# Recurrence scores of two decay steps in one run of TensorE, in a 62,819-instruction two-layer kernel

## The reference, cut to what matters

```python
f = lb + (1.0 - lb) * jax.nn.sigmoid(f_logit)      # decay of each channel, per position
k = 1.0 - f
scores = einsum('bhtd,bhsd,bhtsd->bhts', qc, kc, decay)   # decay = exp(b_t - b_s), b the running sum of log f
o_intra = einsum('bhts,bhsv->bhtv', scores, vc)
o_inter = einsum('bhtd,bhdv->bhtv', qc * exp(b), state)
```

## Time and profile before

| | |
|---|---|
| median of three runs | 3675.24 us |
| the profiled execution, its time | 3676.9 us |
| its span, first to last instruction | 3675.2 us |
| granted clock of PE, mean | 0.996 |
| PE / PEld busy | 3627.0 / 3128.5 us (99% / 85%) |
| DVE, ACT, POOL busy | 2034.2, 1510.6, 685.9 us (55%, 41%, 19%) |
| transfers | 820.57 MB, 223 GB/s in the mean |

### The profile page before, as it was taken

One profiled execution on the slowest core, in us unless ns is written; L12 is line 12 of the kernel. 1 busy time (PEld: TensorE's weight loads), 2 busy tenths in 40 slices (PEclk: granted clock), 3 DMA queues, 4 the chain that ended last, 5 costly groups with the idle time before them and its releaser, 6 DMA issues.

```text
span 3675.2 us, 62819 instructions
## 1 busy us (share of the span) xinstructions
PE 3627.0 (99%) x25608; PEld 3128.5 (85%) x25608; DVE 2034.2 (55%) x3851; ACT 1510.6 (41%) x2753; POOL 685.9 (19%) x407
## 2 busy tenths in 40 slices
PE   9999999999999999999999999999999999999999
PEld 7889888978897988987788788888877899998998
DVE  4757635551645354556645665555566465545555
ACT  3332431231232364576566665444555422223222
POOL 2001130000000000233333321000000254414442
PEclk9999999999999999999999999999999999999999
DMA  8746686557655877866766665554533666666664
GB/s 300 283 180 248 240 302 251 202 211 241 218 218 193 281 255 246 284 229 221 260 230 229 218 240 179 166 169 148 174 139 121 227 247 235 232 233 230 233 236 184
DMA packets 215534, 820.57 MB, mean 223 GB/s; under 512 B 22096, under 2 KB 71504, under 8 KB 152144
## 3 DMA queue, kind: packets, MB, share of 16 engines
q1 hardware_dynamic: 215248, 816.57, 63.1%
HBM read 615.15 MB, written 201.33 MB: 222 GB/s over the span
## 4 chain that ended last, share of the span: by engine, by line
PE 93%; ACT 2%; DVE 2%; DMA 1%; issue 1%; SPq 0%; POOL 0%; DVEq 0%; ACTq 0%
PE bank L1649 89%; PE bank L1653 4%; DVE P L2894 0%; DMA KS<-Kd 0%; ACT slot L2145 0%; SPq L3165 0%; DVE Z1a L2544 0%; ACT L2261 0%; POOL slot L3119 0%; ACT P L2271 0%; DMA Ib<-in_masks_dram 0%; DVE P L2850 0%; DMA DV<-Vd 0%; ACT TP L2281 0%; DVE P L2900 0%
## 5 line engine op out<-in xcount | busy, mean ns | idle before, releaser
L1649 PE MATMUL bank<-slot,Z0b 128*128 128x512 f32 (+1 forms) x3504 | 702.5, 351 | 0.7 <-DVE R L2497 0.7
L1649 PEld LDWEIGHTS bank<-slot,Z0b 128*128 128x128 f32 x3504 | 560.0, 188 | 90.2 <-DVE R L2497 1.5
L1649 PE MATMUL bank<-Z1b,slot 128*128 128x512 f32 (+1 forms) x2568 | 609.9, 381 | 5.3 <-DVE Z1b L2544 5.3
L1649 PE MATMUL bank<-Z1a,slot 128*128 128x512 f32 (+1 forms) x2568 | 607.0, 380 | 6.8 <-POOL slot L3119 5.4
L1649 PEld LDWEIGHTS bank<-Z1a,slot 128*128 128x128 f32 x2568 | 447.5, 190 | 96.5 <-POOL slot L3119 4.5
L1649 PEld LDWEIGHTS bank<-Z1b,slot 128*128 128x128 f32 x2568 | 445.1, 189 | 94.8 <-DVE Z1b L2544 7.4
L3119 POOL TENSOR_TENSOR slot<-raw,slot 128x1024 fp32r<-128x1024 f32 x110 | 274.1, 2498 | 705.5 <-ACT slot L2145 705.3
L2497 DVE SCALAR_TENSOR_TENSOR R<-bank,small,R 128x512 f32<-128x512 f32 x352 | 261.6, 748 | 178.5 <-PE bank L1649 178.1
L2850 DVE TENSOR_SCALAR_CACHE_REDUCE P<-bank 128x512 f32<-128x512 f32 (+3 forms) x320 | 189.3, 608 | 215.5 <-PE bank L1649 214.5
L1649 PE MATMUL bank<-KS,DQ 128*128 128x512 f32 (+3 forms) x960 | 278.1, 388 | 7.5 <-ACT P L2262 3.3
L3137 POOL TENSOR_TENSOR Z0b<-AF,Z0b 128x512 fp32r<-128x512 f32 x88 | 132.7, 1508 | 804.7 <-ACT Z0b L2335 804.7
(11 more groups left out here) (267 smaller groups left out, 5509.0 us busy)
## 6 DMA issues: line engine op xcount, KB each, us to landing
slot<-Wd SPq DMA_DIRECT2D x350, 1024.0 KB, 5.5
Wd<-slot SPq DMA_DIRECT2D x130, 1024.0 KB, 7.7
raw<-in_wts_dram SPq DMA_DIRECT2D x210, 512.0 KB, 4.9
DQ<-Qd SPq DMA_DIRECT2D x192, 128.0 KB, 4.0
slot<-Wd SPq DMA_DIRECT2D x40, 512.0 KB, 6.1
DV<-Vd SPq DMA_DIRECT2D x60, 256.0 KB, 4.6
KS<-Kd SPq DMA_DIRECT2D x24, 512.0 KB, 7.3
KS<-Kd SPq DMA_DIRECT2D x24, 384.0 KB, 7.3
```

Of the source, the lines that this page charges most:

```text
L1649: return e.matmul(o, a, b, start=start, stop=stop, skip_group_check=True)
```

## The change: what it does

Two levels (2p and 2p+1) are now formed in one run p, so a unit has four runs and not eight. To have both levels' operands at once, the second query buffer `Qc` is added, and `Fb` serves as second key buffer once the decays have been used. DVE makes the second level's changed halves straight into the other buffer (`hgrn_decayed`), and ACT copies the two unchanged halves over (two copies per head and run, in runs 0 to 2). The level-0 product of queries and decays moves ahead of the first run. Runs 0 and 2 write banks 2 and 3, runs 1 and 3 banks 4 and 5, each level 128 columns of its own, so the masked copies of a run (`hg m`, `hgrn_merged`) no longer have to be done before the next run, and are placed behind it. ACT's three copies of levels 6 and 7 come together. Space for `Qc` comes from `small` (512 to 360 columns) and from `sg`, which now is the buffer `DG`. In the planner, a run waits for 900 ns of ACT and 2400 ns of DVE for each head. Of the pooling, the second half is now let in 1000 ns after the first half's transfer is expected to be done, where before it was let in when ACT's scaling was.

```diff
         for j in range(2):
-            t[j] = P.put(("hg k", u, j), ("dve", 1400))
-        for i, L in enumerate((0,) + LEVELS):
+            t[j] = P.put(("hg k", u, j), ("dve", 2100))
+        for p in range(4):
             x = max(t)
             yield x
             for j in range(2):
-                t[j] = P.put(("hg sc", u, i, j), ("pe", 400), after=x) + 200
+                t[j] = P.put(("hg sc", u, p, j), ("pe", 800), after=x) + 200
+            if 0 < p < 3:
+                for j in range(2):
+                    yield from self.hgrn_merged(u, p - 1, j)
             for j in range(2):
                 yield t[j]
-                t[j] = P.put(("hg l", u, i, j), ("dve", 2200 if L == 16 else 1350 if L <= 16 else 1050), after=t[j])
+                t[j] = P.put(("hg l", u, p, j), ("act", 900), ("dve", 2400 if p < 3 else 1200), after=t[j])
+            if p == 2:
+                for j in range(2):
+                    yield from self.hgrn_merged(u, p, j)
+                    t[j] = max(t[j], P.clock["dve"])
         yield ("ev", ("A", s, 2 * hp, 1))
         for j in range(2):
             yield t[j]
...
+
+    def hgrn_merged(self, u, p, j):
+
+        yield self.P.end["hg sc", u, p, j] + 200
+        self.P.put(("hg m", u, p, j), ("dve", 1500 if p == 2 else 700), after=self.P.end["hg sc", u, p, j] + 200)
...
             t = P.put(("pl w", s, j), ("dve", 2500 + 1500 * j))
             yield t
             t = yield from self.short(("pl mm", s, j), ("pe", 900), ("act", 690), after=t)
-            self.dma(("Y2 out", s, j), 262144, t)
+            t = self.dma(("Y2 out", s, j), 262144, t)
             P.put(("pl y", s, j))
-            yield t
+            yield t + 1000
...
+        def level_operands(i, j):
+
+            return (Qc if i in (1, 2, 5, 6) else Qb)[j], (Kb if i in (0, 1, 2, 5, 6) else Fb)[j]
+
+        def halves_of(b, L):
+
+            return b[:, :].rearrange("p (n two l) -> p n two l", two=2, l=L)
+
+        def level_scores(i, j):
+
+            w = 64 if i == 7 else 32
+            at = 128 * (i % 2)
+            b = bank[(4 if i // 2 % 2 else 2) + j]
+            return b[:, at:at + NT * w].rearrange("p (c t) -> p c t", c=NT)
...
+            def hgrn_scores(u, p, j):
+                if p == 0:
+                    pe.wait_ge(*dve_hg("hg k", u, j, "q"))
                     pe.wait_ge(*act_g("ev", ("A", u // 2, (24 if u % 2 else 6) + j)))
                     if u:
                         pe.wait_ge(*dve_hg("hg n", u - 1, j, "on"))
                 else:
-                    pe.wait_ge(*dve_hg("hg l", u, i - 1, j, "m" if i - 1 <= 5 else "q"))
-                    if i - 1 > 5:
-                        pe.wait_ge(*act_hg("hg l", u, i - 1, j))
-                for c in range(NT):
-                    if L <= 16:
+                    pe.wait_ge(*dve_hg("hg l", u, p - 1, j, "q"))
+                    pe.wait_ge(*act_hg("hg l", u, p - 1, j))
+                    if p > 1:
+                        pe.wait_ge(*dve_hg("hg m", u, p - 2, j, "1"))
+                    elif u:
+                        pe.wait_ge(*dve_hg("hg yT", u - 1, j))
+                for i in (2 * p, 2 * p + 1) if j == 0 else (2 * p + 1, 2 * p):
+                    q, k = level_operands(i, j)
+                    if i <= 5:
                         pairs = [(32 * g, 32 * g, 32) for g in range(4)]
                     else:
-                        pairs = [(0, 32, 32), (64, 96, 32)] if L == 32 else [(0, 64, 64)]
-                    for ks, qs, w in pairs:
-                        x = mm(A_[ks:ks + w, w * c:w * c + w], Kb[j][:, 128 * c + ks:128 * c + ks + w],
-                               Qb[j][:, 128 * c + qs:128 * c + qs + w], True, True)
-                x.then_inc(*pe_hg.inc("hg sc", u, i, j))
+                        pairs = [(0, 32, 32), (64, 96, 32)] if i == 6 else [(0, 64, 64)]
+                    for c in range(NT):
+                        for ks, qs, w in pairs:
+                            x = mm(level_scores(i, j)[ks:ks + w, c, :], k[:, 128 * c + ks:128 * c + ks + w],
+                                   q[:, 128 * c + qs:128 * c + qs + w], True, True)
+                x.then_inc(*pe_hg.inc("hg sc", u, p, j))
...
+            def hgrn_level(u, p, j):
+                act.wait_ge(*pe_hg("hg sc", u, p, j))
+                if p < 3:
+                    i = 2 * p + 2
+                    act.wait_ge(*dve_hg("hg l", u, p, j, "u"))
+                    (q, k), (q1, k1) = level_operands(i, j), level_operands(i + 1, j)
+                    L = LEVELS[i - 1]
+                    e.activation(halves_of(q1, L)[:, :, 0, :], halves_of(q, L)[:, :, 0, :], ACT.Copy)
+                    e.activation(halves_of(k1, L)[:, :, 1, :], halves_of(k, L)[:, :, 1, :], ACT.Copy).then_inc(
+                        *act_hg.inc("hg l", u, p, j))
                     return
...
+                for i, L, r in (6, 32, 0), (6, 32, 64), (7, 64, 0):
+                    x = e.activation(sv[r:r + L, :, r + L:r + 2 * L], level_scores(i, j)[r:r + L, :, :], ACT.Copy)
+                x.then_inc(*act_hg.inc("hg l", u, p, j))
...
+            def hgrn_decayed(u, i, j):
+
+                L = LEVELS[i - 1]
+                (q, k), (q1, k1) = level_operands(i, j), level_operands(i + 1 if i % 2 == 0 else i, j)
+                tl = tot(u, j, i - 1).rearrange("p (n two) -> p n two", two=2)
+                e.tensor_tensor(halves_of(q1, L)[:, :, 1, :], halves_of(q, L)[:, :, 1, :], bc(tl[:, :, 0], L, 2), ALU.mult)
+                e.tensor_tensor(tot(u, j, i), tl[:, :, 0], tl[:, :, 1], ALU.mult)
+                return e.tensor_tensor(halves_of(k1, L)[:, :, 0, :], halves_of(k, L)[:, :, 0, :], bc(tl[:, :, 1], L, 2), ALU.mult)
+
+            def hgrn_level(u, p, j):
+                dve.wait_ge(*pe_hg("hg sc", u, p, j))
+                if p:
+                    dve.wait_ge(*act_hg("hg l", u, p - 1, j))
+                hgrn_decayed(u, 2 * p + 1, j).then_inc(*dve_hg.inc("hg l", u, p, j, "u"))
+                if p == 3:
+                    return
+                dve.wait_ge(*dve_hg("hg l", u, p, j, "u"))
+                hgrn_decayed(u, 2 * p + 2, j).then_inc(*dve_hg.inc("hg l", u, p, j, "q"))
+
+            def hgrn_merged(u, p, j):
+                cv = Cb[j][:, :, :]
+                dve.wait_ge(*pe_hg("hg sc", u, p, j))
+                dve.wait_ge(*act_c("lmask"))
+                if p:
+                    dve.wait_ge(*dve_hg("hg m", u, p - 1, j, "1"))
+                    x = e.copy_predicated(cv, bc(lmask[:, 2 * p - 1, :], NT), level_scores(2 * p, j))
                 else:
-                    tl = tot(u, j, i - 1).rearrange("p (n two) -> p n two", two=2)
-                    qv = Qb[j][:, :].rearrange("p (n two l) -> p n two l", two=2, l=L)
-                    kv = Kb[j][:, :].rearrange("p (n two l) -> p n two l", two=2, l=L)
-                    e.tensor_tensor(qv[:, :, 1, :], qv[:, :, 1, :], bc(tl[:, :, 0], L, 2), ALU.mult)
-                    e.tensor_tensor(tot(u, j, i), tl[:, :, 0], tl[:, :, 1], ALU.mult)
-                    e.tensor_tensor(kv[:, :, 0, :], kv[:, :, 0, :], bc(tl[:, :, 1], L, 2), ALU.mult).then_inc(
-                        *dve_hg.inc("hg l", u, i, j, "q"))
-                cv = Cb[j][:, :, :]
-                sc = bank[2 + j][:, 0:128].rearrange("p (c t) -> p c t", c=NT)
-                sv = heads_of(Sb[j])
...
+                    x = e.tensor_tensor(cv, level_scores(0, j), id4, ALU.mult)
+                x.then_inc(*dve_hg.inc("hg m", u, p, j, "0"))
+                dve.wait_ge(*dve_hg("hg m", u, p, j, "0"))
+                e.copy_predicated(cv, bc(lmask[:, 2 * p, :], NT), level_scores(2 * p + 1, j)).then_inc(
+                    *dve_hg.inc("hg m", u, p, j, "1"))
+                if p == 2:
+                    sv = heads_of(Sb[j])
+                    dve.wait_ge(*dve_hg("hg m", u, p, j, "1"))
                     dve.wait_ge(*pool_c("zero"))
```

More of the change, by code:

```diff
@@ L1136, in build @@
         lamv = sb("lamv", [128, 8])
-        small = sb("small", [128, 512])
+        small = sb("small", [128, 360])
         raw = [sb(f"raw{i}", [128, 1024]) for i in range(NRAW)]
@@ L1178, in build @@
                    ("lmask", [128, 5, 32], U8)] + two("Cb", [128, NT, 32])
-                  + [x for n in ("Fb", "Kb", "Qb", "Gb", "Sb", "Tb") for x in two(n, [128, SUB])]
+                  + [x for n in ("Fb", "Kb", "Qb", "Qc", "Gb", "Sb", "Tb") for x in two(n, [128, SUB])]
                   + [("Ib", [128, NT, SUB], F32), ("St", [128, 4, 128], F32)] + two("SS", [128, 3, 128])
-                  + [("Hc", [128, 2, HALO + SUB], F32), ("acc", [128, 2, SUB], F32), ("sg", [128, SUB], F32),
+                  + [("Hc", [128, 2, HALO + SUB], F32), ("acc", [128, 2, SUB], F32),
                      ("BG", [128, 2, SUB], F32), ("Vb", [128, NT, 256], F32), ("UG", [128, 2, SUB], F32),
@@ L1336, in build @@
         act_hg = signal("act_hgrn", [x for st in order for x in (
-            [st] if st[0] == "hg kT" or (st[0] == "hg l" and st[2] > 5) else
```

(13 more changed lines are left out.)

53 lines of the change are left out of this document (17 added, 36 removed).

## The result

The kernel after takes 3707.87 us (median of 4 runs, 3701.54 to 3709.61) against 3675.77 of the kernel before beside it: ratio 1.0082 (1.0070 to 1.0094). It is slower by 0.8%; forecast were 3664.5 us, a range of 3656 to 3674, and, with a chance of 0.06, slower.

A forecast was written before the change was run, and what follows sets the result against it. PE, busy 3627.0 of 3675.2 us, was taken to bound the kernel. The terms 9.9 - 1.6 + 0.5 + 1.9 = 10.7 us, off the median 3675.24, gave 3664.5 us, range 3656 to 3674.

The forecast's parts named there:

- Parts 1 and 2: On PE, joining runs saves 32 fixed parts, 9.9 us; 16 width changes inside run 3 cost 0.10 each, 1.6 us.
- rival B: Width changes cost 0.31 us each and a wait for `hg o` replaces the pooling wait: 3669.8 us; chance 0.24.
- Part 3: DVE's level-0 product moves ahead of the first run: cost 0, bounds 0 and 0.7 us per unit.
- part 4: ACT's 96 new copies, 36 us of ACT, stay hidden behind PE's work between runs: cost 0, with 3.4 us of cover.
- Part 5: PE's 4.05 us wait for slot 2's weights falls to some 3.5: gain 0.5 us, half clock afterwards left in.
- C: No half clock after the slot 2 wait (2.8 us) and a later order 4 us better: 3657.7 us; chance 0.12.
- Part 6: PE's 1.88 us wait for the second pooling product goes: gain 1.9 us, bounds 0 to 1.9.
- Part 7: After 1222 us no work changes, but small work lands between other groups: taken as 0, 4 us either way.
- Rival D: PE waits for DVE and ACT ahead of runs; 1 us in each of 24 gaps gives 3688.5 us; chance 0.06.
- E: The later order is worse by 4 us or more: 3669 to 3673 us; chance 0.08.

The follow-up runs named there:

- e9: Joined runs set into the order of before, with 27 small warm-up products shifting PE's stream 108 places; 3676.34 us, ratio 1.0003 to before.
- run 0: Not a follow-up experiment: the first of a unit's four joined runs of scores on PE, forming levels 0 and 1; in unit 0 forecast to start at 33.94 us.
- e2: The kernel after with the pooling edit undone, so the joined runs alone; 3698.94 us, ratio 1.0061 to before.
- e7: The kernel after with 42 small products in PE's warm-up, shifting its instruction stream 168 places; 3697.82 us, ratio 1.0064 to before.
- e8: The kernel after with 16 small products in PE's warm-up, shifting its instruction stream 64 places; 3696.24 us, ratio 1.0060 to before.
- e14: The kernel after with the planner holding recurrence items back 1.6 instead of 1.5 us; 3684.98 us, ratio 1.0022 to before.
- e1: The kernel before with the later pooling step alone; 3672.75 us, ratio 0.9989 to before.
- e3: The kernel after with the planner holding recurrence items back 3.0 instead of 1.5 us; 3708.15 us, ratio 1.0084 to before.
- e10: As e9, but with the 96 copies of 128x256 moved from ACT to DVE and a shift of 124; 3675.85 us, ratio 1.0000 to before.

## Why the prediction was wrong

- Parts 1 and 2 were right: 1.28 us forecast and 1.30 measured for a two-level run, 0.10 and 0.11 around it for 0.10 and 0.10, run 3 at 1.8 for 1.83. Their sum was 8.3 us and measures 8.0; the width changes cost about what was taken, and not rival B's 0.31.
- Part 3 put DVE at 0; in unit 0 the moved product was late by 0.66 us, within the bound of 0.7. The sizes in part 4 held (a copy 0.41 us for 0.37). The conclusion of part 4 failed. It asked whether the next run would wait and found 3.4 us of cover; that was right, for the longest such wait in after is the 0.66 us of part 3. It dismissed what stands behind the waiting copies in one sentence, for evacuations alone. The feature work Z1a and the norm R stand there too. In after PE waited 2.9 us for ACT `R` at 431 us, behind copies for which ACT stood 4.8 us (one DVE instruction ahead of them took 2.63 us, as one in before did at 427 us, without a wait for R), and 2.32 us for Z1a at 799 us. In the old order (e9) two waits for Z1a are 2.32 instead of 1.07: 2.5 us of waits and 3.4 us of half clock.
- Part 5: the wait for slot 2 fell to 3.2 us where 3.5 was forecast, but ended at 51.3 us and not at 50.3, because run 0 began 0.4 us later and held part 3's 0.66 us. No half clock followed it in after, which was part of C. That was luck: in e2, e7, e8 and e14, with 3.3 us of wait there, it did.
- Part 6: the wait did not go. In after PE waited for `PT` 1.4 us. The edit is worth 4 us alone (e1), where this wait went only from 1.88 to 1.50 us; the rest came out elsewhere in the order.
- Part 7 is the step that failed most, and with it the sum: 31 us of loss for 10.7 of gain. It put the redrawn order at 0 with 4 us either way, and only from 1222 us on. In fact the draws measured, with no work changed, lay at +1.5, +40 and +82 us for before and at -23 us for after; of the 22 us that the joined runs lost, 19 went when the old order was kept. A bound worked out from the gaps now there (20 us could turn out otherwise) holds no wait that isn't there yet.
- Missing altogether was the supply of instructions, 8.8 us of waits and two half clocks in after. Rows 2 had the sign of it (issue 0.4): that wait, at 1032 us, stands at place 193 like the others. I read it as noise.
- Rival D had the right kind, waits for DVE and ACT, at the wrong place, ahead of runs; E had the right mechanism at a fraction of its size.
- What stays open: which single moves in the order cost how much in after. Only the sum of them was measured, and 3.4 us of the books have no entry.

## What to carry to other kernels

When a planner sets the order, compare a change at the old order first, and draw a few orders of both kernels: here one number that changes no work moved the time by up to 82 us, eight times the gain sought. Ask of every instruction put into an in-order list what stands behind it when it waits, not only who waits for its result. And count instructions per microsecond: a run that uses up the engine's supply faster than it is refilled stands still at its end, however short its instructions.

## What the runs showed of the hardware that I had not expected

- PE's instructions arrive in packets of 16 KB, 256 each, and the one that is awaited was usable 2.2 to 2.5 us after its packet began. In the six stops of after, e2 and e3 in the table, 128 records with their loads took 4.3 to 5.5 us from the first to where PE went on, where a run of 128 small ones takes 1.3.
- The stop hits whatever stands at that place, as at 207 us in e8, two transposes behind it; and 64 or 168 instructions at the start of the program, 0.1 and 0.3% of PE's, moved the time by 12 and 10 us.
- Waits of 2.1 us and more (788, 790, 1143 us in e9 and e10) were followed by some 3.4 us at 1.2 GHz, a loss of 1.7 us; waits of 0.54 and 1.07 us at the same places were not. The length of the wait alone does not decide it: after's 3.19 us at 51 us and e9's 2.40 us at 2256 us were not followed by any, and e9's 1.75 us at 2141 us was.
